# A hybrid attention and expert-retrieval layer on one core: held-back modulation loads, token tiles taken apart from the output projection on, and a last chunk worked row by row

## What is computed

```python
c_act = jax.nn.silu(c)
mod = (c_act @ w_ada[layer] + b_ada[layer])[:, None, :]
sh1, sc1, gt1, sh2, sc2, gt2 = jnp.split(mod, 6, axis=-1)
h = rmsnorm(x, g_pre_mix[layer]) * (1.0 + sc1) + sh1
y = token_mixer(h, ...)                      # ends in y @ w_out
x = x + gt1 * rmsnorm(y, g_post_mix[layer])
h = rmsnorm(x, g_pre_ffn[layer]) * (1.0 + sc2) + sh2
y = peer_ffn(h, peer_wq[layer], peer_subkeys[layer], peer_u[layer], peer_v[layer])
x = x + gt2 * rmsnorm(y, g_post_ffn[layer])

def peer_ffn(h, w_q, sub_keys, u, v):        # hf: 256 x 1024
    q = (hf @ w_q).reshape(T, PEER_HEADS, 2, PEER_DQ // 2)
    s = jnp.einsum('thcd,hckd->thck', q, sub_keys)
    s1, i1 = lax.top_k(s[:, :, 0], PEER_TOPK)
    s2, i2 = lax.top_k(s[:, :, 1], PEER_TOPK)
    ...                                      # top 16 of the 256 sums, softmax
        act = jax.nn.gelu(jnp.einsum('cd,ced->ce', hc, u[ec]))
        coef = (act.astype(jnp.float32) * wc).astype(hc.dtype)
        return jnp.einsum('ce,ced->cd', coef, v[ec])
```

## Time and profile before

| | |
|---|---|
| runs | 1147.29 us median of 3 (1143.87 to 1148.07) |
| profiled execution | 1147.04 us, span 1144.9 us |
| busy, share of the span | PE 968.0 us (85%), DVE 725.0 (63%), POOL 333.3 (29%), ACT 279.4 (24%) |
| bytes moved | 363.45 MB, 317 GB/s over the span |
| chain that ended last | PE 47%, DMA 40%, DVE 4% |

### The profile page before, as it was taken

One profiled execution on the slowest core, in us unless ns is written; L12 is line 12 of the kernel. 1 busy time (PEld: TensorE's weight loads), 2 busy tenths in 40 slices (PEclk: granted clock), 3 DMA queues, 4 the chain that ended last, 5 costly groups with the idle time before them and its releaser, 6 DMA issues.

```text
span 1144.9 us, 10495 instructions
## 1 busy us (share of the span) xinstructions
PE 968.0 (85%) x3087; PEld 570.0 (50%) x3087; DVE 725.0 (63%) x1892; ACT 279.4 (24%) x755; POOL 333.3 (29%) x324
## 2 busy tenths in 40 slices
PE   5799999998999995888998878877778887876786
PEld 5688888876544754744445423332323333322332
DVE  5699799323465103776686677677677676766553
ACT  3111122234465003232122212212231221221211
POOL 0200001030000000443444554444454444444410
PEclk9999999999999997989999999999888998999988
DMA  9986747875102441599999999999999999999991
GB/s 368 404 326 187 282 157 295 299 214 94 37 19 102 138 153 67 214 423 424 421 423 423 424 421 423 423 422 422 424 424 421 424 422 423 422 423 423 423 420 42
DMA packets 63271, 363.45 MB, mean 317 GB/s; under 512 B 7484, under 2 KB 8140, under 8 KB 30189
## 3 DMA queue, kind: packets, MB, share of 16 engines
q0 software_dynamic: 43136, 292.59, 62.6%
q1 hardware_dynamic: 20076, 70.18, 17.2%
HBM read 361.15 MB, written 1.59 MB: 317 GB/s over the span
## 4 chain that ended last, share of the span: by engine, by line
PE 47%; DMA 40%; DVE 4%; ACT 2%; SPq 2%; issue 2%; POOL 2%; another core or an unknown queue 1%; ACTq 0%; POOLq 0%; DVEq 0%
DMA qk<-in_peer_uv,idx 36%; PE pb L464 22%; PE pb L669 13%; PE pb L495 4%; DMA ring<-in_w_stream 2%; PE pb L615 2%; DMA pair<-in_peer_uv,idx 2%; PE pb L586 2%; DVE qk L1218 2%; POOL qk L434 1%; PE pb L610 1%; DMA arena<-in_w1v 1%; PE pb L568 1%; SPq L346 1%
## 5 line engine op out<-in xcount | busy, mean ns | idle before, releaser
L669 PE MATMUL pb<-arena,sig 128*128 128x512 f32 x424 | 201.0, 626 | 58.0 <-ACT sig L868 58.0
L434 POOL DMA_INDIRECT arena<-in_peer_uv,idx x106 | 126.5, 1193 | 244.8 <-PE pb L669 143.7
L464 PE MATMUL pb<-hT,ring 128*128 128x256 f32 x880 | 190.7, 379 | 0.5 <-ACT arena L729 0.5
L464 PEld LDWEIGHTS pb<-hT,ring 128*128 128x128 f32 x880 | 167.0, 190 | 25.1 <-ACT arena L729 1.7
L1218 DVE CUSTOM_DVE_ANT_0 arena<-arena,sig 128x1024 f32<-128x1024 f32 x106 | 128.4, 1225 | 69.6 <-DMA arena<-in_peer_uv,idx 68.3
L669 PEld LDWEIGHTS pb<-arena,sig 128*128 128x128 f32 x424 | 82.3, 200 | 169.5 <-issue 169.2
L669 PE MATMUL pb<-ring,sig 128*128 128x512 f32 x232 | 123.0, 680 | 31.7 <-ACT sig L868 31.7
L863 ACT ACTIVATE gl<-dot 128x4 f32<-128x4 f32 x64 | 13.1, 205 | 468.3 <-DVE dot L1218 468.3
L669 PEld LDWEIGHTS pb<-ring,sig 128*128 128x128 f32 x232 | 50.9, 224 | 106.5 <-issue 106.5
L434 POOL DMA_INDIRECT ring<-in_peer_uv,idx x58 | 73.6, 1269 | 76.5 <-PE pb L669 71.0
L970 DVE SCALAR_TENSOR_TENSOR y<-arena,cols,y x240 | 95.2, 480 | 0.0
(11 more groups left out here) (219 smaller groups left out, 1193.1 us busy)
## 6 DMA issues: line engine op xcount, KB each, us to landing
ring<-in_w_stream SPq DMA_DIRECT2D x103, 512.0 KB, 4.2
arena<-in_w_ada POOLq DMA_DIRECT2D x32, 512.0 KB, 8.5
arena<-in_w_ada SPq DMA_DIRECT2D x12, 512.0 KB, 13.3
arena<-in_w1k SPq DMA_DIRECT2D x8, 512.0 KB, 5.4
sig<-in_w_ada SPq DMA_DIRECT2D x4, 512.0 KB, 15.3
arena<-in_w1v POOLq DMA_DIRECT2D x1, 2048.0 KB, 8.1
arena<-rev_scratch POOLq DMA_DIRECT2D x16, 128.0 KB, 7.4
arena<-in_peer_uv,idx POOLq DMA_INDIRECT x106
```

Of the source, the lines that this page charges most:

```text
L434: nc.gpsimd.indirect_dma_start(out=rowat[PLACE[n]], out_offset=None, in_=a["peer_uv"], in_offset=bass.IndirectOffsetOnAxis(ap=idx[:, c, e: ...
L464: last = mm(pb[:, bank, 0:SEQ], w[:, k * P:(k + 1) * P], src[:, k, :], start=(k == 0), stop=(k == DT - 1))
L669: last = mm(pb[:, 4 + 2 * t + hf, :], diag[:, c % DEEP, e, :], rowat[PLACE[n]][:, D + hf * 512:D + (hf + 1) * 512], start=(i == 0 and e == ...
```

## The change

Six edits, in the order of the program.

1. SP loads c before x; ACT evaluates silu first, then loads the table of the root, and only tile 0's squares of x are ACT's, tile 1's are DVE's.
2. POOL's 32 modulation loads wait until slab 7 has landed (`ring_in[ROUND - 1]`), and DVE runs each part one step later: parts 2 and 3 in the loop, 4 and 5 behind it.
3. The output projection is made for token tile 0 first. Norms, transposes, queries and scores of m = 0 to 3 are done for each token tile apart (`STEPS`: eight steps of one tile, then twelve for both); ten steps (`EARLY`) come before the first chunk. The query tiles take other places in the ring, and two of the row places wait for other releases (`OUT_FREE`, `QUERY_FREE`); the four late places come at row 92. The root's table is loaded behind the attention.
4. The parts of `retrieve` come a chunk later (b = 1 to 3 of four), the softmax's sum before a unit's first dots, and gelu's table is loaded behind the first exp.
5. In the last chunk gelu, product and diagonal matrix are made for each row by itself (`shares_of`).
6. The last root's table is loaded before it is waited for, and x is made and stored in two halves of 512 columns.

```diff
-M_FIRST = 8
-SOON, SLOTS, LATE = 12, 16, 76
-RING_FREE = 9
+SOON, SLOTS, LATE = 12, 16, 92
+OUT_FREE, QUERY_FREE = 10, 11
+STEPS = [(m, (0,)) for m in range(4)] + [(m, (1,)) for m in range(4)] + [(m, (0, 1)) for m in range(4, 2 * PH)]
+SCORED = [[1 + min(i for i, (mm, ts) in enumerate(STEPS) if mm == m and t in ts) for m in range(2 * PH)]
+          for t in range(TT)]
+EARLY = 10
...
-        s = n % RING if later < 0 else (7, 4, 5, 6)[later % 4]
+        m = n - T_WQ
+        s = n % RING if m < 0 else (7, 0, 1, 2, 3, 6)[m] if m < 6 else (7, 0, 1, 6)[(m - 6) % 4]
...
+def shares_of(c):
+    return [(s, s + 1) for s in range(CH)] if c == TT * CPT - 1 else [(0, CH)]
...
+            sp.dma_start(cact, a["c"].partition_broadcast(P)).then_inc(s_c, 16)
             sp.dma_start(x[:, :, :], a["x"].rearrange("(t p) d -> p t d", p=P)).then_inc(s_x, 16)
-            sp.dma_start(cact, a["c"].partition_broadcast(P)).then_inc(s_c, 16)
...
+                for hf in range(2):
+                    sp.wait_ge(v_out, 2 * t + hf + 1)
+                    sp.dma_start(out[t * P:(t + 1) * P, hf * 512:(hf + 1) * 512],
+                                 x[:, t, hf * 512:(hf + 1) * 512]).then_inc(o_done, 16)
...
+            g.wait_ge(ring_in[ROUND - 1], 16)
             for i in range(2, 6):
                 for k in range(8):
                     g.wait_ge(ada_used, i * 8 + k - 7)
...
-                if n == RING_FREE:
+                if n == OUT_FREE:
+                    g.wait_ge(ring_used, T_WQ)
+                if n == QUERY_FREE:
                     g.wait_ge(ring_used, T_WQ + 5)
...
+            def out_part(t, k):
+                tile = T_OUT + k
+                if t == 0:
+                    pe.wait_ge(v_m, k + 1)
+                    pe.wait_ge(ring_in[SLOT[tile]], 16 * TURN[tile])
+                for hf in range(2):
+                    last = mm(pb[:, 2 + 2 * t + hf, :], y[:, k, t * P:(t + 1) * P],
+                              ring[:, SLOT[tile], hf * 512:(hf + 1) * 512], start=(k == 0), stop=(k == DT - 1))
+                return last
...
+            def query_columns(i):
+                m, ts = STEPS[i]
+                if i >= 2:
+                    pe.wait_ge(a_q, i - 1)
+                if len(ts) == TT:
+                    column_tile(i % 2, T_WQ + m, h2T)
+                    return
+                pe.wait_ge(ring_in[SLOT[T_WQ + m]], 16 * TURN[T_WQ + m])
+                for k in range(DT):
+                    last = mm(pb[:, i % 2, 0:P], ring[:, SLOT[T_WQ + m], k * P:(k + 1) * P],
+                              h2T[:, k, ts[0] * P:(ts[0] + 1) * P], start=(k == 0), stop=(k == DT - 1))
+                last.then_inc(ring_used if ts[0] else p_q, 1)
...
+            for k in range(DT):
+                last = out_part(0, k)
+            last.then_inc(p_out, 1)
+            for k in range(4):
+                out_part(1, k).then_inc(ring_used, 1)
+            h2_transposes(0)
...
+            query_columns(0)
+            query_columns(1)
+            subkey_scores(0)
+            subkey_scores(1)
+            for k in range(4, DT):
+                out_part(1, k).then_inc(ring_used, 1)
...
+            h2_transposes(1)
+            pe.wait_ge(a_h2T, 4)
+            for i in range(4, EARLY):
+                query_columns(i)
+                if i > 4:
+                    subkey_scores(i - 1)
+            subkey_scores(EARLY - 1)
             for c in range(TT * CPT):
                 expert_chunk(c)
...
             act.wait_ge(s_c, 16)
             fn(cact, cact, ACT.Silu).then_inc(a_c, 1)
+            act.wait_ge(g_const, 4)
+            fn(turned[:, :], eps[:, :], ACT.Sqrt).then_inc(a_turn, 1)
+            act.wait_ge(s_x, 16)
+            fn(xs[:, 0, :], x[:, 0, :], ACT.Square, accum_out=ss[:, 0:1]).then_inc(a_ss, 1)
...
+            fn(turned[:, :], eps[:, :], ACT.Sqrt).then_inc(a_turn, 1)
...
+            def out_norm(t):
                 if t:
-                    act.wait_ge(v_sc, 1)
+                    act.wait_ge(ring_used, T_WQ)
+                else:
+                    act.wait_ge(p_out, 1)
...
+                for f, (lo, hi) in enumerate(shares_of(c)):
+                    act.wait_ge(v_dot, c * CH + hi)
+                    fn(gl[:, b, lo:hi], dot[:, b, lo:hi], ACT.Gelu_apprx_tanh).then_inc(a_gl, 1)
+                    act.wait_ge(v_cf, c + f + 1)
+                    for s in range(lo, hi):
+                        fn(diag[:, b, s, :], ident[:, :], ACT.Copy, scale=cf[:, b, s:s + 1]).then_inc(a_dg, 1)
...
+            for i in range(4, EARLY):
+                query_out(i)
+                if i > 4:
+                    score_out(i - 1)
+                if i == EARLY - 2:
                     unit_exp(0)
+                    gelu_next()
...
+            dve.wait_ge(s_x, 16)
+            V_.tensor_tensor_reduce(out=xs[:, 1, :], in0=x[:, 1, :], in1=x[:, 1, :], scale=1.0, scalar=0.0,
+                                    op0=ALU.mult, op1=ALU.add, accum_out=ss[:, 1:2]).then_inc(a_ss, 1)
...
-            ada_part(2, ada_more, 0)
...
-                ada_part(r + 3, ada_more, r + 1)
+                ada_part(r + 2, ada_more, r)
             ch.leave(2)
+            ada_part(4, ada_more, 2)
...
+            for part in range(3):
+                retrieve(0, part)
+            token_norms(1)
+            for part in range(3):
+                retrieve(1, part)
...
                 if b == 0:
                     softmax_sum(k)
+                for f, (lo, hi) in enumerate(shares_of(c)):
+                    for s in range(lo, hi):
...
+                if b and k + 2 < UNITS:
+                    retrieve(k + 2, b - 1)
```

More of the change, by code:

```diff
@@ L672, in expert_chunk, with subkey_scores @@
                     last.then_inc(p_row_used, 1)
[L675 to L682 removed]
+            def subkey_scores(i):
+                m, ts = STEPS[i]
+                pe.wait_ge(a_q, i + 1)
+                if i >= 2:
+                    pe.wait_ge(a_s, i - 1)
+                for t in ts:
+                    last = mm(pb[:, 2 + i % 2, t * NK:(t + 1) * NK], query[:, m % 4, t * P:(t + 1) * P],
@@ L876, in query_out @@
-            def query_out(m):
-                act.wait_ge(ring_used, T_WQ + m + 1)
-                fn(query[:, m % 4, :], pb[:, m % 2, 0:SEQ], ACT.Copy).then_inc(a_q, 1)
-            for m in range(M_FIRST):
-                query_out(m)
-                if m == 1:
-                    score_out(0)
-                    score_out(1)
-                if m > 2:
-                    score_out(m - 1)
-                if m == M_FIRST - 2:
+                for f, (lo, hi) in enumerate(shares_of(c)):
[4 more added lines that the diff above has]
+                        fn(diag[:, b, s, :], ident[:, :], ACT.Copy, scale=cf[:, b, s:s + 1]).then_inc(a_dg, 1)
@@ new lines, in score_out, with query_out @@
+            def score_out(i):
+                m, ts = STEPS[i]
+                act.wait_ge(p_sc, i + 1)
+                fn(ssb[:, ts[0]:ts[-1] + 1, m, :],
+                   pb[:, 2 + i % 2, ts[0] * NK:(ts[-1] + 1) * NK].rearrange("p (t k) -> p t k", k=NK),
+                   ACT.Copy).then_inc(a_s, 1)
+            def query_out(i):
+                m, ts = STEPS[i]
+                if ts == (0,):
+                    act.wait_ge(p_q, i + 1)
+                else:
+                    act.wait_ge(ring_used, T_WQ + m + 1)
+                fn(query[:, m % 4, ts[0] * P:(ts[-1] + 1) * P], pb[:, i % 2, 0:len(ts) * P], ACT.Copy).then_inc(a_q, 1)
@@ L1202, in finish_tile @@
                                          rows[3], ALU.mult))
-                dve.wait_ge(a_std, 4 + t)
+                dve.wait_ge(a_std, 6 + t)
                 ch.link(V_.reciprocal(rstd[:, 6 + t:7 + t], std[:, 6 + t:7 + t]))
-                V_.scalar_tensor_tensor(out=x[:, t, :], in0=scaled[1], scalar=rstd[:, 6 + t:7 + t], in1=x[:, t, :],
-                                        op0=ALU.mult, op1=ALU.add).then_inc(v_out, 1)
-                dve.wait_ge(v_out, t + 1)
-            for k in range(2):
-                for part in range(3):
-                    retrieve(k, part)
+                for hf in range(2):
+                    cs = slice(hf * 512, (hf + 1) * 512)
+                    V_.scalar_tensor_tensor(out=x[:, t, cs], in0=scaled[1][:, cs], scalar=rstd[:, 6 + t:7 + t],
+                                            in1=x[:, t, cs], op0=ALU.mult, op1=ALU.add).then_inc(v_out, 1)
@@ L1212, in _ @@
+                dve.wait_ge(v_out, 2 * (t + 1))
+            for part in range(3):
[3 more added lines that the diff above has]
+                retrieve(1, part)
             for c in range(TT * CPT):
                 k, b = divmod(c, SEG)
-                for s in range(CH):
-                    n = c * CH + s
-                    u = rowat[PLACE[n]][:, 0:D]
-                    dve.wait_ge(row_in[PLACE[n]], landed(n))
-                    V_.tensor_tensor_reduce(out=u, in0=u, in1=h2[:, c // CPT, :], scale=1.0,
```

(2 more changed lines are left out.)

196 lines of the change are left out of this document (95 added, 101 removed).

## The result

| | before | changed |
|---|---|---|
| median (range), 4 runs each | 1146.4 us (1143.87 to 1148.07) | 1117.55 us (1115.45 to 1119.28) |
| profiled execution, span | 1147.04, 1144.9 us | 1119.28, 1117.5 us |

The ratio is 0.9725 (95% interval 0.970 to 0.975), some 31.5 us. It is an estimate of its own: the two medians alone divide to 0.9748, 28.9 us. The forecast was 1112 us, range 1106 to 1123, which was 35.3 us under the median of the first three runs (1147.29). The profiled execution of the changed kernel was the slowest of its four. I cut both traces at the same six events; each row is the time in us since the event above it (the first since the start).

What follows compares the result with a forecast made beforehand. DMA at 423 GB/s sets the pace once rows are asked for; before that, PE's program and a chain of small steps. Head 10.0, middle 18.0 and tail 7.9 sum to 35.9: 1147.04 to 1111.1, stated as 1112 us, range 1106 to 1123.

Steps and rivals of the forecast that it cites:

- Head, forecast 10.0: Start to first column tile: holding POOL's loads lets slab 7 land earlier; tile at 43.5 instead of 53.55; range 7 to 11.
- PE's last round takes 3.6 us ... and the first column tile starts 0.46 behind it, at 43.5: Last modulation round: slab 7 lands at 38.7, DVE ends 0.7 later, PE's round takes 3.6 us instead of 5.11.
- The give-back at 207: Rival at the channel mean: DVE or SP late after parts 4 and 5, PE waits 8 us: 1120; chance 0.10.
- the pressure on DVE: Parts 4 and 5 back to back: channel sum near 200, PE asks at 207; priced nothing, low end 4 us.
- Middle, forecast 18.0: Projection to rows: first row 22.7 us earlier, minus 3.7 for three query tiles, minus 1.0 for a gap; range 14 to 20.
- query block of one tile: Before the first row: eight products of 128 columns on PE at 0.305 us each, 2.44 us; low end 1.73.
- the 1.0 us for it: Allowance for a DMA gap before row 12, if PE's first expert product comes late; range 0 to 6 us.
- rival of rows run dry: PE's first expert product comes at 485 instead of 477, so the DMA rests 8 us: 1120; chance 0.17.
- Tail, forecast 7.9: After the last landing: 7.0 from the last chunk by rows, 0.4 from the root, 0.5 from halved x and store.
- the first three are worked while the last one is under way: Last chunk: only one row left after the last landing, so PE ends 4.0 us behind it instead of 11.1; gain 7.0.
- 6.1 for a last row at half clock: Tail: the gain from the last chunk by rows if the last row too is at half clock, instead of 7.0 us.
- 0.4 + 0.5: End of the kernel: 0.4 us for the root and its hand-over, 0.5 for x and its store in halves.

Runs made afterwards that it cites:

- again: The changed kernel with nothing altered, run once more: 1115.43 us, ratio 0.9717 to the kernel before.
- l_whole: The changed kernel with the last chunk worked as a whole again, none row by row: 1116.88 us, ratio 0.9723 to the kernel before.
- h_only: The kernel before with edits 1 and 2 alone (c first, loads held, DVE's parts one step later): 1142.37 us, ratio 0.993.
- l_four: The changed kernel with the last four chunks row by row instead of the last one: 1113.34 us, ratio 0.9695 to the kernel before.
- r_early: The changed kernel with the parts of retrieve put back behind chunks b = 0 to 2: 1113.75 us, ratio 0.9688 to the kernel before.
- l_four_2: The changed kernel with the last four chunks row by row, measured once more: 1111.64 us, ratio 0.9689 to the kernel before.
- m_only: The changed kernel without edits 1, 2, 5 and 6, so edits 3 and 4 alone: 1125.5 us, ratio 0.9788 to the kernel before.
- h_free: The changed kernel without the wait that holds back POOL's modulation loads: 1124.41 us, ratio 0.9786 to the kernel before.
- e_whole: The changed kernel with edit 6 undone, x made and stored whole: 1117.59 us, ratio 0.9729 to the kernel before.

## Why the prediction was right, and where its steps were not

**Head, forecast 10.0.** The mechanism was right: 9.1 us in the profile and in again, 7.0 to 9.4 in all executions with the hold and c first. The step "PE's last round takes 3.6 us ... and the first column tile starts 0.46 behind it, at 43.5" has PE ready for its last round when slab 7 and hT(7) are. Slab 7 landed at 40.1 instead of my 38.7, and in six of these nine executions PE's own pass ended last: its eight rounds, without a gap, took 28.0 to 30.2 us. In l_whole and h_only the tile came 1.8 to 2.0 us later still (46.52, 46.27) though slab 7 was there at 41.0 and 40.9: the pass took 30.2 and 30.0 us. The forecast had no term for PE's own pass. In the other three the last wait was the forecast's, hT(7) from DVE, only with later loads: 0.21 us of it in l_four, 1.23 in r_early and in l_four_2, whose timeline has

```profile
41.28 3.69 PE L507 MATMUL pb<-hT,ring 128*128 128x256 f32 x16 [1.23 <-DVE hT L1036]
```

The give-back at 207 did not happen: the channel sum was done 1.5 us before PE turned to the mean. I had priced the pressure on DVE at nothing, and that was right, but close.

**Middle, forecast 18.0.** Measured 24.8 − 3.6 = 21.3 in the profiles, 24.4 (22.1 to 26.7) by m_only. The first row came 24.8 us nearer to the projection instead of 22.7. The mis-sized terms: the query block of one tile, priced at 2.44, took 1.84 (3.68 for the two up to the scores), and transposes with copies 1.8 instead of 2.6; norms took 7.14 (forecast 7.2, though the terms that I gave for it add up to 7.0). PE's first expert product stood 29.3 us behind the first row (forecast 30.9), and the windows show no gap, so the 1.0 us for it was not needed; the rows took 2.8 to 3.8 us longer, which three more query tiles at 1.24 us account for. The rival of rows run dry fell with that.

**Tail, forecast 7.9.** Here a step failed, "the first three are worked while the last one is under way". It looked at DVE and ACT and forgot what PE had in hand. A whole chunk's products begin 2.3 us after its last landing, so when the chunk before the last is whole, PE has eight rows of 1.75 us from there; the last landing follows 9.8 us after that chunk's, and PE ends 2.3 + 14.0 − 9.8 = 6.5 us behind it. Measured: 6.5 where PE runs at full clock (h_free, r_early, again), 8.2 where the first eight of its records take 5.37 us (e_whole), 9.5 where they take 6.69 (the changed kernel). The last chunk whole takes 9.4 to 9.7 where it runs at full clock (h_only, m_only, l_whole), so edit 5 is worth 3 us, and nothing where the backlog runs at half; not 7. The medians of l_whole and again (0.9723 and 0.9717) can't tell 0 from 3. The tail of the earlier trace rows was 11.1, with the last chunk's first records at 5.37 us: a bad draw, which made the gain look larger. The 4.2 that is near the forecast's 4.0 was measured with four chunks. The forecast's 6.1 for a last row at half clock was too high as well: it allows the row 0.9 us more than at full clock, but two rows took 6.69 us in the changed kernel, 3.3 each, and with that the gain is 5.5. The end behind the squares was right: 0.9 for 0.4 + 0.5.

**What the sum left out.** The attention took 140.5 us in the execution of the kernel before that my sum was made against, and 140.0 to 146.1 in the others: a forecast made against one profiled execution inherits its draws. Short attention there hid 5.4 us of the change's gain in the profiled pair, and the long tail added 1.7. The terms themselves come out at 9.1 + 21.3 + 4 (tail: 3 and 0.9) = 34.4 instead of 35.9, since the middle's surplus of 3.3 nearly pays for the tail's missing 4. That is luck: both lie outside the ranges that I had given them (14 to 20 and 6.9 to 8.2), with opposite signs. The measured median lies in the stated range, but 0.6 above my own of 1107 to 1117; the medians, 1117.55 and 1115.43, are 3 to 6 us above 1112. How much of the rest is the attention's clock can't be split further, since runs of one kernel spread over up to 10 us.

## What to carry to other kernels

Work that is split at the end of a pipeline gains only if the engine behind it is free by then: count the backlog of the last engine from the chunk before, and split so many chunks that it is gone, with the engine's lower clock in mind. A transfer held back moves the bound to the next thing in the chain (here PE's own pass, and then each microsecond in front of it counts, as the order of two small loads showed). Before a term is read as "what this stretch costs", look whether the clock there is the same in a second execution.
